# A hybrid decoder step on one core: the MLP's down product in token pieces of 512, 512 and 32 columns in place of three of 352

## The reference

```python
def conv_ffn(h, buf, w_gate, w_up, conv_w, conv_b, w_down):
    T = h.shape[1]
    a = h @ w_gate
    ext = jnp.concatenate([buf.astype(a.dtype), a], axis=1)
    c = conv_b + sum(conv_w[j] * ext[:, j:j + T] for j in range(CONV_W))
    y = (jax.nn.silu(c) * (h @ w_up)) @ w_down
    return y, ext[:, -(CONV_W - 1):]
```

## Time and profile before

| | us |
|---|---|
| timed runs: median of 2 (lowest, highest) | 1605.48 (1602.06, 1608.9) |
| the profiled execution's own time | 1599.84 |
| its span, first to last instruction | 1598.1 |

### The profile page before, as it was taken

One profiled execution on the slowest core, in us unless ns is written; L12 is line 12 of the kernel. 1 busy time (PEld: TensorE's weight loads), 2 busy tenths in 40 slices (PEclk: granted clock), 3 DMA queues, 4 the chain that ended last, 5 costly groups with the idle time before them and its releaser, 6 DMA issues.

```text
span 1598.1 us, 24365 instructions
## 1 busy us (share of the span) xinstructions
PE 1502.4 (94%) x9601; PEld 1420.8 (89%) x9601; DVE 925.6 (58%) x1505; ACT 493.6 (31%) x964; POOL 507.9 (32%) x238
## 2 busy tenths in 40 slices
PE   6699899899989997879999999999999999999998
PEld 4698788798978886749999999999999999999998
DVE  5537455744574457646467475665747566474744
ACT  4446454644564455245341010101101011110111
POOL 0111221141114111313208264361725436173520
PEclk9799999999999899979999999999999999999998
DMA  5312012100310030726102020101202010120102
GB/s 196 135 54 67 14 29 83 51 27 16 95 40 27 16 94 30 227 63 199 46 15 88 32 80 27 53 26 53 66 14 79 26 53 27 53 66 27 53 0 109
DMA packets 121483, 98.16 MB, mean 61 GB/s; under 512 B 4422, under 2 KB 111175, under 8 KB 121288
## 3 DMA queue, kind: packets, MB, share of 16 engines
q1 hardware_dynamic: 119280, 88.39, 18.0%
q10 hardware_dynamic: 2136, 8.86, 1.4%
HBM read 77.71 MB, written 19.52 MB: 61 GB/s over the span
## 4 chain that ended last, share of the span: by engine, by line
PE 53%; DMA 1%; issue 0%; SPq 0%; ACT 0%; POOL 0%; ACTq 0%; DVE 0%
PE f_dn L1980 5%; PE f_dn L1981 5%; PE f_gp L272 5%; PE f_dn L1982 5%; PE f_up L272 5%; PE f_gp L274 5%; PE f_gp L273 5%; PE f_up L273 5%; PE f_up L274 5%; PE f_up L1882 2%; PE f_up L1883 2%; PE f_up L1884 2%; DMA m_raw<-w_out 1%; PE f_gp L2011 0%; PE f_dn L1949 0%
## 5 line engine op out<-in xcount | busy, mean ns | idle before, releaser
L264 POOL TENSOR_TENSOR m_hi<-m_raw,ones 128x1024 fp32r<-128x1024 f32 x66 | 162.5, 2462 | 446.9 <-PE f_gp L274 278.1
L272 PE MATMUL z_ps<-h_hi,w_hi 128*128 128x352 f32 x672 | 229.9, 342 | 14.6 <-DVE h_lo L295 10.2
L274 PE MATMUL z_ps<-h_hi,w_lo 128*128 128x352 f32 x672 | 220.2, 328 | 0.0
L273 PE MATMUL z_ps<-h_lo,w_hi 128*128 128x352 f32 x672 | 220.0, 327 | 0.0
L2288 DVE TENSOR_TENSOR room<-room,f_dn 128x352 f32<-128x352 f32 x264 | 137.6, 521 | 119.9 <-PE f_dn L1982 119.9
L265 POOL TENSOR_TENSOR m_lo<-m_raw,m_hi 128x1024 fp32r<-128x1024 f32 x66 | 186.0, 2818 | 5.2
L1980 PE MATMUL f_dn<-f_ahi,m_hi 128*128 128x352 f32 x528 | 172.4, 326 | 3.7 <-issue 3.7
L272 PE MATMUL f_gp<-f_hi,m_hi 128*128 128x352 f32 x528 | 172.4, 327 | 0.5 <-DVE room L2175 0.5
L634 POOL TENSOR_TENSOR w_lo<-w_raw,w_hi 128x1024 fp32r<-128x1024 f32 x28 | 66.7, 2380 | 330.3 <-ACT w_hi L1098 330.3
L1981 PE MATMUL f_dn<-f_alo,m_hi 128*128 128x352 f32 x528 | 171.0, 324 | 0.0
L1982 PE MATMUL f_dn<-f_ahi,m_lo 128*128 128x352 f32 x528 | 170.9, 324 | 0.0
(11 more groups left out here) (303 smaller groups left out, 3054.7 us busy)
## 6 DMA issues: line engine op xcount, KB each, us to landing
w_raw<-w_in SPq DMA_DIRECT2D x28, 512.0 KB, 3.9
m_raw<-w_gate SPq DMA_DIRECT2D x22, 512.0 KB, 3.9
m_raw<-w_up SPq DMA_DIRECT2D x22, 512.0 KB, 4.0
m_raw<-w_down SPq DMA_DIRECT2D x22, 512.0 KB, 5.3
x_d<-room ACTq DMA_DIRECT2D x1, 4224.0 KB, 12.6
room<-x_d SPq DMA_DIRECT2D x3, 1408.0 KB, 7.6
room<-x_prompt SPq DMA_DIRECT2D x8, 512.0 KB, 6.5
s_kp<-cache_k SPq DMA_DIRECT2D x16, 256.0 KB, 3.0
```

Of the source, the lines that this page charges most:

```text
L264: link(nc.gpsimd.tensor_tensor(hi, raw, ones.rearrange("p (o c) -> p o c", o=1).broadcast_to(list(raw.shape)), ALU.mult))
L272: nc.tensor.matmul(out, whi[:, k, :], hi[:, k, :], start=(k == 0), stop=False)
L273: nc.tensor.matmul(out, whi[:, k, :], lo[:, k, :], start=False, stop=False)
L274: last = nc.tensor.matmul(out, wlo[:, k, :], hi[:, k, :], start=False, stop=(k == chunks - 1))
```

## The change

The down product no longer uses `piece(n)` but a cut of its own, at 0, 512, 1024 and 1056 tokens. Both `down_unit` functions and the count of pieces that an output tile waits for follow it. The branches, the convolution and the norm keep the three pieces of 352. The number of units, matmuls and evictions is the same, and so is the order of instructions on every engine.

```diff
+DOWN = [0, T // 2, T, TT]
+
+
+def down_piece(n):
+    return slice(DOWN[n], DOWN[n + 1])
...
                     pe.wait_ge(dn_free[b], dn_use(g, False, first + j // 2))
-                    out = dn[b][:, 0:PW]
+                    out = dn[b][:, 0:DOWN[n + 1] - DOWN[n]]
                     for c in range(G2):
                         w = f"d{c}"
-                        nc.tensor.matmul(out, whi[w][:, d, :], ahi[c][:, piece(n)], start=(c == 0), stop=False)
-                        nc.tensor.matmul(out, whi[w][:, d, :], alo[c][:, piece(n)], start=False, stop=False)
-                        last = nc.tensor.matmul(out, wlo[w][:, d, :], ahi[c][:, piece(n)], start=False, stop=(c == G2 - 1))
+                        nc.tensor.matmul(out, whi[w][:, d, :], ahi[c][:, down_piece(n)], start=(c == 0), stop=False)
+                        nc.tensor.matmul(out, whi[w][:, d, :], alo[c][:, down_piece(n)], start=False, stop=False)
+                        last = nc.tensor.matmul(out, wlo[w][:, d, :], ahi[c][:, down_piece(n)], start=False, stop=(c == G2 - 1))
...
-                        pieces = min(-(-(i + 1) * P // PW), NPC)
+                        pieces = len([first for first in DOWN[:NPC] if first < (i + 1) * P])
...
-                    v.tensor_tensor(acc[:, d, piece(n)], acc[:, d, piece(n)], dn[b][:, 0:PW], ALU.add).then_inc(dn_free[b], 1)
+                    v.tensor_tensor(acc[:, d, down_piece(n)], acc[:, d, down_piece(n)], dn[b][:, 0:DOWN[n + 1] - DOWN[n]], ALU.add).then_inc(dn_free[b], 1)
```

## The result

| | us |
|---|---|
| before: median of 2 runs (lowest, highest) | 1605.48 (1602.06, 1608.9) |
| after: median of 2 runs (lowest, highest) | 1682.11 (1676.75, 1687.46) |
| ratio after / before, 95% interval | 1.0477 (1.0305 to 1.065) |
| the profiled execution after, its span | 1687.46, 1685.7 |

The account below looks back on a forecast made before the run. PE was taken to bound the kernel; 71.2 us in the loop stages plus 4.0 in the last made 75.2, giving 1675.1 on the profiled time or 1680.7 on the median, so 1678 us, range 1646 to 1692.

Parts of the forecast that it names:

- both terms: Sum of the forecast: ten loop down stages of eight chunks, 71.2 us more, and the last down stage, 4.0 us more.
- The wait: Loop down stages: PE awaits the second wide unit's eviction, covered only by a 0.67 us narrow unit; chain 1.05 us.
- the 0.08 us to spare: Kernel before: each eviction was said to end 0.08 us before the weight load that reuses its bank.
- the rival of a dear narrow fp32r matmul: Narrow matmuls cost what wide ones do, 227 ns: about 1706 to 1711 us; chance 0.04.
- The mis-sized term: a wide matmul: Down product: a 512-column matmul takes 226.8 ns, with ends of 213.3 and 232.9; a wide unit 1.361 us.
- The step that failed: the last stage: Last down stage, piece by piece: no waits, 4.0 us more stream, half-clock start and clock rows as before.
- the clock against the loop stages: Rival: granted clock falls to half in loop down stages, up to 265 us more; chance 0.03.
- No stall: Rival: the narrow unit covers the eviction, only the stream grows, 44.5 us: 1644 to 1650 us; chance 0.09.
- Pace per instruction: Rival: down matmuls cost 160 ns whatever their width: about 1605 to 1610 us; chance 0.04.

## Why the prediction was right, and where it was off

The forecast, slower by 75.2 us, came out at 76.6 by the first medians. So close a hit is in part luck: those are medians of two runs each, and five runs against nine gave 81.9. By the traces the loop stages cost 75 us and the last stage 5 to 8.5, so 80 to 83 in sum, and both terms were put too low. By the forecast's steps:

*The wait.* The chain was put at 0.20 + 0.69 + 0.05 + 0.11 = 1.05 us from the second wide unit's end to the next one's pace. In the profile after, an output chunk takes 3.82 us and its twelve wide matmuls 12 x 0.231 = 2.77, which leaves 1.05. With DVE's add shortened and PE's instructions the same, the wait is gone. One reading was too generous: of the 0.08 us to spare in the kernel before, the 0.05 from DVE's end to PE's load have to go off, so 0.03 are left. The narrow matmuls cost 111 ns, as the f32 rows had it, so the rival of a dear narrow fp32r matmul falls.

*The mis-sized term: a wide matmul.* 226.8 ns was chosen from 213.3 to 232.9, on the argument that the surcharge does not grow with the columns. Measured are 231 ns. Twelve of them make 0.05 us per chunk, 4 us over 80 chunks: the loop stages cost 75 us and not 71.2. Why the surcharge is larger at 448 and 512 columns than at 352 no run shows. The Trainium skill's gap of N/2.4 + 2.5 ns ("TensorE: Matmul & The Clock Gate", "Back-to-back issue gap") would be 215.8 here, further off.

*The step that failed: the last stage.* "The last stage runs piece by piece ... so nothing waits" held, and so, nearly, did its 4.0 us of stream. That its clock stays as it was did not: within or right at the end of the run of eight narrow units a new stretch at half clock begins, of 10.2 or 3.4 us, which costs 0.5 to 4.5 us on top of the stream. The prediction had weighed the clock against the loop stages, where it stayed at 1.00 as forecast, and not against the one place where eight narrow units follow each other.

*The rivals.* No stall: 27.57 us a stage is what it would have been, but the stall is there. Pace per instruction: 448 columns cost 204 ns and 512 cost 231, so pace goes with columns.

Between the first two profiles the span differs by 87.6 us: 75 in the loop stages, 8.5 in the last one, 1 between the stages, and 3.2 ahead of the first down stage, which starts at 888.1 us and not at 884.9. The code ahead of it is the same in all the kernels, and in the ten profiles that start lies between 884.9 and 894.4 us, so the 3.2 us are no more than profiles differ by there anyway. What makes them differ was not examined.

## What to carry to other kernels

With two accumulator banks each eviction is covered by exactly one unit of matmuls, so each eviction must be compared with the unit that PE does right behind its own, not by sums: equal pieces were just long enough here, and unequal ones with the same totals stalled. A remainder piece of a few columns costs its weight loads, and a run of such pieces can cost the clock too, although PE counts as busy. Cut tokens into equal pieces unless wide matmuls have been measured to be cheaper per column. A third bank, which would give each eviction two units as cover, was not tried.

## What the runs showed of the hardware that was not expected

- The surcharge of an fp32r matmul over one column a cycle is 13 ns at 256 and 352 columns, and 17 and 18 ns at 448 and 512.
- Narrow fp32r matmuls with 128 x 128 weights start 111 ns apart at full clock and 213 at half clock (1636.44 to 1637.08 is three of them). At full clock that is the pace of the matmuls of 4 columns in the earlier trace rows too.
- With the narrow matmuls gathered, the granted clock fell to 0.50 in or right behind their run in all ten loop stages of one kernel, in the first after 5.2 us in which PE counts as busy for 4.99. With narrow units between wide ones it stayed at 1.00 in the loop stages.
- A short DVE add, 0.29 us by its row, delayed the add behind it by 0.21 us only.
